# Second block's projections: sums of squares in four column strips of the array, inverse lengths spread from two row strips

## The reference

```python
h = rms_norm_2(x, norm1_gain[l]) * (1.0 + sc1) + sh1
z = h @ w_in[l]
(c_q, c_kv, k_pe, q_n, k_c, v_c, k_s, v_s, k_w, v_w,
 g_nsa, g_mla_merge, g_nsa_merge) = jnp.split(z, split_at, axis=-1)
q = (rms_norm_2(c_q, q_a_gain) @ w_q_b).reshape(B, S, MLA_HEADS, MLA_QK)
kv = (rms_norm_2(c_kv, kv_a_gain) @ w_kv_b).reshape(B, S, MLA_HEADS, MLA_NOPE + MLA_V)
q = rms_norm_2(q, q_gain)     # per head, 64 + 32 features
k = rms_norm_2(k, k_gain)     # per head, 64 + 32 shared features
q = partial_rope(rms_norm_2(q, q_gain), cos_t, sin_t)   # NSA: 8 heads of 64
```

## Time and profile before

| | us |
|---|---|
| median of 3 runs | 5055.8 |
| runs | 5047.97, 5055.8, 5056.52 |
| span of the profiled execution | 5047.9 |
| PE busy | 4667.6 (92%) |
| DVE busy | 2748.2 (54%) |

### The profile page before, as it was taken

How to read it: one execution, slowest core, us unless ns; L and a number is a source line. 1 busy time by engine, 2 the same in 40 slices (tenths; PEclk the granted TensorE clock), 3 DMA queues, 4 the chain that set the end, 5 groups by cost and what they waited for, 6 DMA issues and landing times. The chain is left out here.

```text
span 5047.9 us, 87945 instructions
## 1 busy us (share of the span) xinstructions
PE 4667.6 (92%) x37909; PEld 3587.9 (71%) x37932; DVE 2748.2 (54%) x3731; ACT 1104.4 (22%) x1515; POOL 777.1 (15%) x684
## 2 busy tenths in 40 slices
PE   9997999999888999889968899998979989999999
PEld 7776888999766767645456677765545568888887
DVE  5776554444446788578876692333653334442432
ACT  2443222222303232111113211112222222100000
POOL 0000432112001165000001010012010000330330
PEclk9998999999899999999989999999999999999999
DMA  3444321222221334512221251246230024113112
GB/s 134 154 163 159 87 63 48 67 64 65 71 91 62 114 141 169 223 61 84 100 97 55 98 193 46 88 130 145 52 70 6 9 95 132 62 42 110 58 54 97
DMA packets 221412, 474.37 MB, mean 94 GB/s; under 512 B 34983, under 2 KB 101480, under 8 KB 220516
## 3 DMA queue, kind: packets, MB, share of 16 engines
q1 hardware_dynamic: 176340, 337.92, 21.1%
q0 software_dynamic: 33392, 117.54, 6.8%
q10 hardware_dynamic: 11296, 13.27, 0.7%
HBM read 328.01 MB, written 138.16 MB: 92 GB/s over the span
## 5 line engine op out<-in xcount | busy, mean ns | idle before, releaser
L5136 PE MATMUL tail_product<-tail_x_hi,tail_w_hi 128*128 128x512 f32 x832 | 329.6, 396 | 12.0 <-DVE tail_x_lo L184 10.7
L5136 PE MATMUL tail_product<-tail_x_lo,tail_w_hi 128*128 128x512 f32 x832 | 325.2, 391 | 0.0
L5136 PE MATMUL tail_product<-tail_x_hi,tail_w_lo 128*128 128x512 f32 x832 | 324.4, 390 | 0.0
L3807 PE MATMUL win_product<-kept_hn_hi,win_w_hi 128*128 128x512 f32 x560 | 230.2, 411 | 8.8 <-DVE kept_hn_lo L3961 6.3
L1817 PE MATMUL front_product<-kept_x_hi,front_w_hi 128*128 128x512 f32 x544 | 220.9, 406 | 9.9 <-DVE kept_x_lo L184 9.7
L3807 PE MATMUL win_product<-kept_hn_hi,win_w_lo 128*128 128x512 f32 x560 | 220.6, 394 | 0.0
L3807 PE MATMUL win_product<-kept_hn_lo,win_w_hi 128*128 128x512 f32 x560 | 220.6, 394 | 0.0
L1817 PE MATMUL front_product<-kept_x_hi,front_w_lo 128*128 128x512 f32 x544 | 213.8, 393 | 0.0
L2848 PE MATMUL oproj_product<-kept_mix_hi,oproj_w_hi 128*128 128x512 f32 x512 | 205.6, 402 | 8.6 <-DVE kept_mix_lo L184 8.6
L1817 PE MATMUL front_product<-kept_x_lo,front_w_hi 128*128 128x512 f32 x544 | 213.3, 392 | 0.0
L2848 PE MATMUL oproj_product<-kept_mix_hi,oproj_w_lo 128*128 128x512 f32 x512 | 200.9, 392 | 0.0
(11 more groups left out here) (759 smaller groups left out, 11065.3 us busy)
## 6 DMA issues: line engine op xcount, KB each, us to landing
s_decayed<-front_ring SPq DMA_DIRECT2D x96, 256.0 KB, 4.0
tail_w<-in_w_gu SPq DMA_DIRECT2D x44, 512.0 KB, 3.3
second_raw<-in_w_in SPq DMA_DIRECT2D x35, 512.0 KB, 3.6
front_w<-in_even_w SPq DMA_DIRECT2D x34, 512.0 KB, 3.9
s_pm<-kept_begun SPq DMA_DIRECT2D x64, 256.0 KB, 2.1
kept_hn_hi_plain<-s_pm SPq DMA_DIRECT2D x16, 1024.0 KB, 10.0
win_cq_hi_plain<-in_ada_w POOLq DMA_DIRECT2D x16, 1024.0 KB, 5.4
oproj_ring<-in_odd_w POOLq DMA_DIRECT2D x30, 512.0 KB, 3.8
```

Source lines behind the costliest of these rows:

```text
L3807: mm = pe.matmul(pp[:, u, h, :], l, b, start=(k == 0 and m == 0), stop=(k == depth(s) - 1 and m == 2))
L5136: mm = pe.matmul(pp[:, s % 2, h_, :], l, b, start=(k == 0 and m == 0), stop=(k == deep(s) - 1 and m == 2))
```

## The change

`total` now makes four products of 256 tokens instead of two of 512. Each of the four token quarters has a matrix of 32 columns and writes its own 32 partitions of `win_mean` (32 q to 32 q + 31), which occupies its own 32-column strip of the array. `win_mean` is now 128 x 256: rows 32 q + r hold head r for quarter q. The `ckv` sums are unchanged (`mean`).

`take_root` and the root on ACT then handle 128 x 256 instead of 12 (8) x 1024. `invert_heads` makes four reciprocals of 32 x 256, each to another place: quarters 0 and 1 go to partitions 0 to 31, quarters 2 and 3 to partitions 32 to 63, both in columns 512 to 1023. The two parts are then formed as 64 x 512. In `spread_out` the first half of the tokens is read from partitions 0 on and the second half from partitions 32 on; `win_spread` carries its rows twice, at 0 and at 32. The four products of a spread are ordered upper part for both halves, then lower part for both halves.

```diff
-                    for h in range(2):
-                        mm = pe.matmul(out[:, h, :], w, src[rows_, h * H2:(h + 1) * H2], start=first, stop=last)
+                    for q in range(4):
+                        mm = pe.matmul(pm[32 * q:32 * q + 32, :], w, src[rows_, q * QW:(q + 1) * QW], start=first, stop=last)
...
-                    for h in range(2):
-                        for n, part in enumerate((ri, ri_lo)):
-                            mm = pe.matmul(pb[:, h, :], r(spread[0:rows_, col:col + P]), r(part[0:rows_, h * H2:(h + 1) * H2]),
-                                           start=(n == 0), stop=(n == 1))
+                    for n, part in enumerate((ri, ri_lo)):
+                        for h in range(2):
+                            own = slice(32 * h, 32 * h + rows_)
+                            mm = pe.matmul(pb[:, h, :], r(spread[own, col:col + P]), r(part[own, H2:T]), start=(n == 0), stop=(n == 1))
...
-                def take_root(src, eps, rows_):
-                    dve.tensor_scalar(rt[0:rows_, :], src, eps, None, ALU.add).then_inc(root, 1)
+                def take_root(eps):
+                    dve.tensor_scalar(rt[:, 0:QW], pm[:, :], eps, None, ALU.add).then_inc(root, 1)
+
+                def invert_heads(n, base):
+
                     dve.wait_ge(rooted, n)
-                    ch(dve.reciprocal(rt[0:rows_, :], rt[0:rows_, :]))
-                    if n != ROOT_CKV:
-                        ch(upper(dve, ri[0:rows_, :], rt[0:rows_, :]))
-                        ch(lower(dve, ri_lo[0:rows_, :], rt[0:rows_, :], ri[0:rows_, :]))
+                    for q in range(4):
+                        row, col = 32 * (q // 2), H2 + QW * (q % 2)
+                        dve.reciprocal(rt[row:row + 32, col:col + QW], rt[32 * q:32 * q + 32, 0:QW]).then_inc(inv, 1)
+                    dve.wait_ge(inv, base + 4)
+                    ch = Chain(dve, inv, base + 4)
+                    ch(upper(dve, ri[0:64, H2:T], rt[0:64, H2:T]))
+                    ch(lower(dve, ri_lo[0:64, H2:T], rt[0:64, H2:T], ri[0:64, H2:T]))
```

More of the change, by code:

```diff
@@ L3564, in prep_constants @@
     p = np.arange(P)
[L3565 to L3575, removed]
+    w = np.zeros((P, 180), f)
+    w[p, 10 + p // 64] = 1 / 64
+    w[p, 48 + p // 64] = 1 / 96
+    w[p, 84 + p // 32] = 1 / 96
+    w[:, 116:124] = RMS_EPS / 768
+    w[64:96, 148:156] = 1 / 96
+    s = np.zeros((64, T), f)
+    for h in (0, 32):
+        for j in range(6):
+            s[h + 2 * j + p // 64, P * j + p] = 1
+        for j in range(2):
+            s[h + 4 * j + p // 32, 768 + P * j + p] = 1
     return {"prep_sum": w, "prep_spread": s}
@@ L3711, in _, with total, mean @@
                 r = lambda t: t.bitcast(F32R)
-                def total(out, w, done, first, last, rows_=slice(0, P), src=None):
+                def total(w, done, first, last, rows_=slice(0, P), src=None):
                     src = sq if src is None else src
-                    for h in range(2):
-                        mm = pe.matmul(out[:, h, :], w, src[rows_, h * H2:(h + 1) * H2], start=first, stop=last)
+                    for q in range(4):
+                        mm = pe.matmul(pm[32 * q:32 * q + 32, :], w, src[rows_, q * QW:(q + 1) * QW], start=first, stop=last)
                     if done:
                         mm.then_inc(summed, 1)
+                def mean(first, last):
+                    for h in range(2):
+                        mm = pe.matmul(pb[:, h, :], avg[:, :], sq_half(h), start=first, stop=last)
+                    mm.then_inc(summed, 1)
                 def sum_squares(s):
@@ L3830, in gained, with sqrt @@
                     act.activation(out, p, ACT.Identity, scale=gains[:, col:col + 1], bias=0.0).then_inc(evac, 1)
-                def sqrt(n, rows_):
+                def sqrt(n, width=QW):
                     act.wait_ge(root, n)
-                    act.activation(rt[0:rows_, :], rt[0:rows_, :], ACT.Sqrt).then_inc(rooted, 1)
+                    act.activation(rt[:, 0:width], rt[:, 0:width], ACT.Sqrt).then_inc(rooted, 1)
                 act.wait_ge(ahead.gain_in, 32)
@@ L3990, in _ @@
                         dve.wait_ge(summed, 6)
-                        take_root(flat(pm)[0:12, :], RMS_EPS, 12)
+                        take_root(RMS_EPS)
                     if 1 <= s <= 6:
@@ L4014, in _ @@
                     if s == 20:
[L4015 removed]
+                        invert_latent(INV_N)
                         for n in range(2):
@@ L4030, in _ @@
                         dve.wait_ge(summed, sums[at[("kn", 3)]] + 1)
-                        take_root(flat(pm)[0:8, :], RMS_EPS, 8)
+                        take_root(RMS_EPS)
                     if s == 39:
-                        invert(ROOT_K, 8, INV_Q)
+                        invert_heads(ROOT_K, INV_Q)
                     for n in {41: (0, 1), 43: (2, 3)}.get(s, ()):
```

45 lines of the change are left out of this document (24 added, 21 removed).

## The result

The changed kernel takes 5022.9 us in the median of 4 runs (5015.61 to 5027.27), the kernel before 5056.16 (5047.97 to 5057.69, 4 runs); the ratio is 0.9938, with an interval of 0.9924 to 0.9952. Forecast were 5025.3 us and a range of 5013 to 5041. The profiled execution has a span of 5019.4 us, against 5047.9.

The account below looks back on a forecast made before the run. PE was taken as the bound from 3026 us on, DVE as deciding in slots 1 to 9; 2.5 + 1.8 + 20.7 + 5.5 = 30.5 us off 5055.8 gave 5025.3, range 5013 to 5041.

Parts of the forecast that it names:

- (a): Slots 1 to 9: DVE sets the pace, so the first spread comes 2.5 us earlier, not 7.3.
- (b): The six n spreads: 0.46 us saved on four, lost on two where DVE is just in time; 1.8 us stays.
- (c): From 3026 us on, PE bound: 17 sums save 20.7 us and 12 spreads 5.5 us.
- (d): Constants some 260 KB larger at the stage's start: covered while PE waits for DVE, else up to about 1 us; taken as 0.
- rival 5: PE's new waits in slots 1 to 9 lower its clock; first spread up to 1 us later, 5026 to 5027; inside forecast.
- Rival 1: Narrow sums: only two strips run at a time, a sum 1.3 us, saving 23.0 us, 5033 us; chance 0.13.
- Rival 2: Narrow sums: program order holds strips back, five steps instead of two, saving 18.8 us, 5037 us; chance 0.06.
- The prediction's own row: Trace row of 16 records at 91.98, 1.03 us in all; program order was said to need 1.2 and more.
- Rival 3: Narrow sums: column strips do nothing; only chain and spreads save, 8.6 us, 5047 us; chance 0.06.
- Rival 4: Narrow sums and spreads: each change of strip drains the array, some 0.15 us; 27 us slower, 5083 us; chance 0.05.

Follow-up runs that it names:

- eight_in_turn: The changed kernel with each narrow sum as eight products of 128 tokens, the four strips in turn, twice; a sum 0.892 us, stage 528.5 us against 528.3.
- one_strip: The kernel before with each narrow sum cut in four products of 256 tokens, all in one column strip; stage 556.4 us against 557.9.
- the three orders: Three variants of the changed kernel: spread products half by half; sums in eight products, strip by strip or in turn; stages 528.3, 529.1 and 528.5 us.
- both: The changed kernel with DVE's modulation turns moved and one shorter reciprocal plus a copy; stage 521.8 us, median 5013.13 us, ratio 0.9928 to the kernel before.
- turns_moved: The changed kernel with another table of DVE's modulation turns, slots 3 to 6 having one each; stage 526.3 us against 528.3.
- halves_outside: The changed kernel with a spread's products ordered upper and lower part of the first half, then of the second; stage 528.3 us, as in the changed kernel.
- two_strips: The changed kernel with halves of 512 tokens in two column strips instead of quarters in four, and one reciprocal; stage 535.8 us against 528.3.

## Why the prediction was right, by its steps

The time between the first product and the three marks of the stage, against the sum of the prediction:

| step | forecast | measured | from |
|---|---|---|---|
| (a) slots 1 to 9, to the first spread | 2.5 | 0.9 | 124.10 - 123.19 |
| (b) the six `n` spreads | 1.8 | 1.85 | 42.12 - 40.27, from first spread to first `cq` sum |
| (c) sums and spreads behind | 26.2 | 26.8 | 391.69 - 364.88, from there to the last product |
| (d) constants | 0 | 0 | nothing left for it in the three, see below |
| sum | 30.5 | 29.6 | 557.9 - 528.3 |

**Sums and spreads (c).** Four strips at a time, taken at 0.9 a sum, measured 0.89; the saving is 1.24 and not 1.22, on 17 sums. The spreads' 0.46 was 0.465. Here PE is busy in 228.00 of 228.00 and 112.00 of 112.00 us, and all of it comes off the end.

**The six spreads (b).** Of six, the fourth and sixth took 1.40 and 1.44 and still kept DVE's pace, as forecast for two of them; the earlier trace rows was the right place to look.

**Slots 1 to 9 (a).** The reasoning on DVE was right by the terms: weights 1.15 earlier (1.2 forecast), the root 0.79 less (0.8), the splits 0.78 less (0.8), the reciprocals 0.52 more (0.35). DVE was done with the chain 2.2 earlier in the stage. (The 2.06 of the prediction runs to the start of the spread; the splits themselves ended 0.10 before it, 1.96 behind the reciprocal, and took 1.18 now.) The waits of 2 and 3 us came: 2.17 and 2.87. What failed is the clock, rival 5. Behind the second wait it fell for 3.4 us, which costs PE 1.6 to 1.7 us; so PE came to the first spread at 123.2, when DVE's chain had ended at 121.8. Without the fall PE would have been there at 121.5 and the spread would have come some 0.1 behind the chain, as before: 121.9, an estimate, and (a) would be 2.2. I had put this fall at "up to 1" and left it out of the sum; it belonged in it, at 1.3. That a chain on DVE shorter by 5 us changed nothing shows that it was PE's way and no longer DVE's.

**The constants (d).** The three steps begin at the stage's first product and can't show a delay ahead of it. But the stage begins at 2862.5 us in `eight_in_turn`, with the larger constants, and at 2862.6 in `one_strip`, with the small ones, so none is to be seen there either.

**The rivals.** Rival 1 is excluded by 0.89 against the 1.30 of two strips. Rival 2 by the three orders. The prediction's own row against it was weaker than it says: counted from the first record, a sum has 0.09 at its edge, so nine steps give some 1.06 against the 1.03 of the row, and not 1.2 and more. And its price of 0.57 a sum doesn't fit its own 1.5 a sum, which is 0.63 less than 2.13. It was the runs that decided. Rival 3 and the thought that small records would help by the quarters in one strip, 2.15. Rival 4, a drain at each change of strip, by the same 0.89: eight records go from strip to strip, 16 do so at 0.892, and no 0.15 a change is to be seen.

**The time.** The stage's 29.6 us explain the 33.3 between the medians (5056.16 - 5022.9) up to 3.7. I didn't find a place for these 3.7, and they are within what the other stages vary from run to run: in the other group of runs, that of `both`, the same two kernels lie 27.7 apart (5047.36 - 5019.65), below the 29.6. The forecast of 5025.3 also met two errors of opposite sign, 1.6 too much in (a) and 0.6 too little in (c). That a sum from one execution may be taken off a median holds here, as the stage's length doesn't vary: 528.34 and 528.35 in two executions of the changed kernel whose spans are 5019.4 and 5037.8.

## What to carry to other kernels

A narrow product whose output has 32 partitions or fewer uses a quarter of the array's columns: cut its streamed side in four and put the quarters in four strips, whose records need no particular order. What follows such a result works on all four strips at once for the price of its columns, as long as it doesn't handle them one by one. Where the engine that feeds PE decides, first ask what fills that engine ahead of the data, and count in the sum that a new wait of PE can be followed by some us at half the clock; a wait moved to another place, as in `turns_moved`, can give back most of what its removal brought (5.2 of 7.3 us).

## What the runs showed of the hardware

- Eight plain fp32 records of 256 columns take 2.14 us in one strip and 0.89 in four, and the same work in two strips takes 1.30; the edges are 0.42 with one strip, 0.44 with two and 0.46 with four. So beside each other the strips cost at most 0.04 us.
- The order of issue between strips is nearly free: 0.912 against 0.892 for 16 records, 0.985 against 0.978 for the F32R spreads in two strips of rows. A product can start ahead of an earlier one that reads another strip (2993.00 against 2993.33 in `halves_outside`).
- A reciprocal on DVE costs by its columns and not by its partitions: 1.75 us for 128 x 256, 7.05 / 4 = 1.76 for 32 x 256, 3.34 for 64 x 512 in `two_strips`, 6.53 for 12 x 1024.
- Whether the clock falls behind a wait isn't told by the wait's length: a wait of 2.17 us was followed by a granted clock of 1.00, one of 1.36 us by 0.56, one of 2.87 us by a fall of 3.4 us in the changed kernel and another of 2.87 us by one of 6.8 us in `turns_moved`. What else decides it stays open. In three kernels 3.4 us more of the lower level cost 1.6 us.
- A split of 128 x 1024 on DVE took 1.23 us by itself and 3.73 to 3.79 with a multiply of POOL wholly beside it, before and after.
